# A transformer layer with PEER experts: the first 768 columns of `expert_v` multiplied densely with scattered weights, on one stream of 1280-column rows

## The reference

```
def peer_ffn(h, w_q, sub_keys_1, sub_keys_2, expert_u, expert_v):
    ...
    s1 = jnp.einsum('bshd,hnd->bshn', q[..., 0, :], sub_keys_1.astype(f32))
    s2 = jnp.einsum('bshd,hnd->bshn', q[..., 1, :], sub_keys_2.astype(f32))
    v1, i1 = lax.top_k(s1, PEER_TOPK)
    v2, i2 = lax.top_k(s2, PEER_TOPK)
    cand = (v1[..., :, None] + v2[..., None, :]).reshape(B, S, PEER_HEADS, PEER_TOPK * PEER_TOPK)
    ...
    top, pos = lax.top_k(cand, PEER_TOPK)
    eidx = jnp.take_along_axis(cidx, pos, axis=-1)
    gate = jax.nn.softmax(top, axis=-1)
    ...
        u = jnp.take(expert_u, idx, axis=0)
        act = jax.nn.gelu(jnp.einsum('td,tkd->tk', h_t, u), approximate=False)
        vv = jnp.take(expert_v, idx, axis=0)
        return jnp.einsum('tk,tkd->td', g * act, vv)
```

## Time and profile before

| | us |
|---|---|
| median of three runs | 2214.85 |
| the profiled execution | 2217.75 |
| its span | 2216.0 |
| VectorE busy | 1599.2 (72%) |
| TensorE busy | 1398.2 (63%) |
| POOL busy | 656.1 (30%) |
| ScalarE busy | 352.1 (16%) |
| DMA | 680.99 MB, mean 307 GB/s |

### The profile page before, as it was taken

How to read it: one execution, slowest core, us unless ns; L and a number is a source line. 1 busy time by engine, 2 the same in 40 slices (tenths; PEclk the granted TensorE clock), 3 DMA queues, 4 the chain that set the end, 5 groups by cost and what they waited for, 6 DMA issues and landing times.

```text
span 2216.0 us, 20313 instructions
## 1 busy us (share of the span) xinstructions
PE 1398.2 (63%) x7103; PEld 1192.1 (54%) x7103; DVE 1599.2 (72%) x2429; ACT 352.1 (16%) x702; POOL 656.1 (30%) x707
## 2 busy tenths in 40 slices
PE   4799999999998989999999990399000000000000
PEld 3688888888885468888888880398000000000000
DVE  5936555655664023777778669988899998999998
ACT  2022222222221011011111110276000000000000
POOL 1021332223321001333332446422433333333331
PEclk8889999999999999999999995699555555555555
DMA  9936554565455552799999999854999999999995
GB/s 397 385 132 242 228 196 177 213 254 226 175 191 226 214 206 94 292 344 360 361 357 357 363 407 411 328 149 125 422 422 421 422 422 421 422 422 422 422 422 243
DMA packets 122001, 680.99 MB, mean 307 GB/s; under 512 B 13488, under 2 KB 13616, under 8 KB 65840
## 3 DMA queue, kind: packets, MB, share of 16 engines
q0 software_dynamic: 73728, 419.46, 47.0%
q1 hardware_dynamic: 47760, 257.97, 30.5%
q10 hardware_dynamic: 416, 2.25, 0.2%
HBM read 675.44 MB, written 4.19 MB: 307 GB/s over the span
## 4 chain that ended last, share of the span: by engine, by line
PE 37%; DMA 30%; DVE 28%; issue 2%; ACT 1%; POOL 1%; DVEq 0%; ACTq 0%; POOLq 0%
DVE ps L1569 15%; DMA arena<-in_u_rows,arena 15%; DMA arena<-in_expert_v,arena 13%; PE ps L865 13%; PE ps L1186 5%; PE ps L914 5%; PE ps L943 4%; DVE arena L1523 3%; DVE arena L1235 2%; PE ps L1084 2%; PE ps L948 2%; DMA arena<-in_ada 1%; PE ps L957 1%; DVE arena L1463 1%; DVE arena L1458 1%
## 5 line engine op out<-in xcount | busy, mean ns | idle before, releaser
L1569 DVE SCALAR_TENSOR_TENSOR ps<-arena,ps 128x2048 f32<-128x2048 f32 x256 | 602.8, 2355 | 36.1 <-DMA arena<-in_expert_v,arena 5.7
L1158 PE MATMUL ps<-arena 128*128 128x256 f32 x1792 | 386.9, 379 | 0.0
L544 POOL DMA_INDIRECT arena<-in_u_rows,arena x256 | 245.9, 961 | 446.8 <-DVE arena L1523 393.1
L1158 PEld LDWEIGHTS ps<-arena 128*128 128x128 f32 x1792 | 340.4, 190 | 46.2
L544 POOL DMA_INDIRECT arena<-in_expert_v,arena x256 | 239.8, 937 | 410.5 <-DVE ps L1569 380.0
L865 PE MATMUL ps<-arena 128*128 128x256 f32 x1440 | 341.2, 381 | 2.8 <-DMA arena<-in_w_in 2.8
L1523 DVE SCALAR_TENSOR_TENSOR arena<-arena,ps 128x1152 f32<-128x1152 f32 x208 | 279.5, 1354 | 77.9 <-DMA arena<-in_u_rows,arena 73.4
L865 PEld LDWEIGHTS ps<-arena 128*128 128x128 f32 x1440 | 263.0, 191 | 33.0 <-issue 3.2
L1186 PE MATMUL ps<-arena 128*128 128x128 f32 x512 | 124.8, 399 | 88.6 <-DVE ps L1531 86.1
L1186 PEld LDWEIGHTS ps<-arena 128*128 128x128 f32 x512 | 98.8, 206 | 93.1 <-DVE ps L1531 86.3
L1214 DVE SCALAR_TENSOR_TENSOR arena<-arena 128x2048 f32<-128x2048 f32 x60 | 142.8, 2380 | 0.0
(11 more groups left out here) (246 smaller groups left out, 1579.1 us busy)
## 6 DMA issues: line engine op xcount, KB each, us to landing
arena<-in_ada SPq DMA_DIRECT2D x96, 1024.0 KB, 4.9
arena<-in_u_dense SPq DMA_DIRECT2D x128, 448.0 KB, 6.9
arena<-in_w_in SPq DMA_DIRECT2D x45, 1024.0 KB, 6.7
arena<-in_w_tail SPq DMA_DIRECT2D x32, 1024.0 KB, 6.9
arena<-in_w_in SPq DMA_DIRECT2D x12, 512.0 KB, 16.9
arena<-in_u_rows,arena POOLq DMA_INDIRECT x256, 9.0
arena<-in_expert_v,arena POOLq DMA_INDIRECT x256, 25.5
arena<-in_x ACTq DMA_DIRECT2D x1, 2048.0 KB, 15.0
```

Of the source, the lines that this page charges most:

```text
L544: nc.gpsimd.indirect_dma_start(out=row, out_offset=None, in_=table[:, :], in_offset=bass.IndirectOffsetOnAxis(ap=i32(idx[:, b, k:k + 1]), ...
L1158: last = mm(bank(5 + j % 2, 0, T), u_tile[j % len(u_tile)][:, k, :], h2T[:, k, :], start=(k == 0), stop=(k == KU - 1))
L1569: stt(sums_ps, v_row[n % len(v_row)], wv[:, b, k:k + 1], sums_ps, ALU.mult, ALU.add).then_inc(v_sum, 1)
```

## The change

`expert_v` gets what `expert_u` had. Its first 768 columns (`VD`) become 128 tiles of 128 experts, which are multiplied for all experts and both blocks (`v_product`, L1352 of the kernel after). For this the weights of a token's chosen experts must stand in an array over all 128 x 128 experts; they are scattered there by one-hots: for a token, the one-hot of its first keys times the weighted one-hot of its second keys, a matmul over the 128 places (`scatter`, L1327), four tokens a step in 64 steps `s`. ScalarE writes the result over `dense`, whose products of `u` for those tokens have been used (`scattered`, L843). For even `s` the first keys' one-hot is made by POOL (`nc.gpsimd.tensor_tensor`, L602) and two passes of ScalarE (L850, L852), for odd `s` by VectorE (L1730); the second keys' weighted one-hots are VectorE's, four instructions (L1733).

`KU` goes from 7 to 6, and `u` rows and `v` rows both have 1280 columns (`GU`) and share one stream of 512 rows through six slots (`ROWS`). The tiles too are one stream. Dots take `h` from SBUF throughout (L1701). Two dots stand in 10 of 14 gaps inside each of the last seven routes. The token step is turned round: `dense[:, :, t]` is now the weights and the one-hot the moving operand (L1289), so that tokens' products come out with the 128 places along the free axis; VectorE compares the second keys (spread as well, 256 columns instead of 128) and multiplies in one instruction of 128x512 (L1709), and TensorE sums over the partitions (`sum_up`, L1301). Per step stand two dots. From step 36 on (`HALF` + `LAG`) the scatters of block 0 run beside the steps of block 1. The sums of `v`'s rows are kept in SBUF (L1749).

```
@@ @@
-        hot = [view(repl_at, 4, P), view(repl_at + 4 * P, 4, P)]
...
+        row_slot = [new(GU) for _ in range(ROWS)]
...
+        h_row = [view(KU * T + b * GU, GU) for b in range(TB)]
+        v_acc = h_row
...
@@ @@
-            for j in range(4, NKEYS):
-                sp.wait_ge(tile_ps, j - 3)
+            for j in range(4, 2 * NKEYS):
+                sp.wait_ge(tile_ps, NKEYS if j in (NKEYS, NKEYS + 1) else j - 3)
+                if j == NKEYS + 2:
+                    sp.wait_ge(w_ps, T // 4)
                 product_tile(j)
...
@@ @@
+            for s in range(T // 4):
+                rows_to(rows_at_scatter(s))
+                if s == 0:
+                    pool.wait_ge(idxT_out, 1)
+                    pool.wait_ge(tile_ps, NKEYS)
+                if on_vector(s):
+                    continue
+                if s >= 2:
+                    pool.wait_ge(w_ps, s - 1)
+                nc.gpsimd.tensor_tensor(first_hot[s % 2], every_key(), first_keys(s), ALU.subtract).then_inc(key_gap, 1)
+            rows_to(2 * TB * KTOP)
...
@@ @@
+            def wanted(q):
+
+                if q >= 2:
+                    pe.wait_ge(prod_out, q - 1)
+                pe.wait_ge(hot_out, 2 * q + 2)
+                for i in range(4):
+                    last = mm(bank(4 + q % 2, i * P, (i + 1) * P), dense[:, :, 4 * q + i], hot[q % 2][:, i, :], start=True, stop=True)
+                last.then_inc(y_ps, 1)
...
+            def scatter(s):
+
+                if on_vector(s):
+                    pe.wait_ge(hot1_vec, s // 2 + 1)
+                else:
+                    pe.wait_ge(hot1_act, 2 * by_act(s))
+                pe.wait_ge(hot2_out, 4 * (s + 1))
...
+                if s >= 1:
+                    pe.wait_ge(w_out, s if s <= HALF else s - 1)
+                for i in range(4):
+                    last = mm(bank(scatter_bank(s), i * P, (i + 1) * P), first_hot[s % 2][:, i, :], second_hot[s % 2][:, i, :], start=True, stop=True)
+                last.then_inc(w_ps, 1)
...
             spread_keys(0)
             for q in range(T // 4):
                 if q + 1 < T // 4:
                     spread_keys(q + 1)
...
+                wanted(q)
+                if q:
+                    sum_up(q - 1)
...
+                if q >= HALF + LAG:
+                    scatter(q - HALF - LAG)
...
+            pe.wait_ge(w_out, T // 4)
+            for j in range(NKEYS):
+                pe.wait_ge(tile_land[place(NKEYS + j)], 16 * ((NKEYS + j) // len(tile_slot) + 1))
+                last = v_product(j, 0)
...
@@ @@
+            def wanted_products(q):
+
                 dve.wait_ge(y_ps, q + 1)
+                if q >= 2:
+                    dve.wait_ge(summed, q - 1)
+                dve.wait_ge(key2_out, q + 1)
+                stt(prod[q % 2], key2_h[q % 2], plus_p, bank(4 + q % 2).rearrange("p (a b) -> p a b", a=4),
+                    ALU.is_equal, ALU.mult).then_inc(prod_out, 1)
...
+            for q in range(HALF, 2 * HALF):
+                wanted_products(q)
+                if q == HALF + 1:
+                    activations(0)
+                more_dots(1)
...
+                if q >= HALF + LAG:
+                    weighted_one_hot(q - HALF - LAG)
+                if ndot[0] < TB * KTOP:
+                    more_dots(1)
+                else:
+                    v_sums(1)
...
+            for s in range(HALF, 2 * HALF):
+                weighted_one_hot(s)
+                if s % 2:
+                    v_sums(1)
```

More of the change, by code:

```diff
@@ new lines, in first_key @@
+            def first_key(s):
+                n = by_act(s)
+                act.wait_ge(key_gap, n)
+                nc.scalar.activation(first_hot[s % 2], first_hot[s % 2], ACT.Abs).then_inc(hot1_act, 1)
+                act.wait_ge(hot1_act, 2 * n - 1)
+                nc.scalar.activation(first_hot[s % 2], first_hot[s % 2], ACT.Relu, bias=ones[:, 0:1], scale=-1.0).then_inc(hot1_act, 1)
+            for q in range(T // 4):
+                one_hot(q)
+                if q == 0:
+                    act.wait_ge(idxT_ps, 1)
+                    nc.scalar.activation(idxT.rearrange("p a b -> p (a b)"), bank(7), ACT.Copy).then_inc(idxT_out, 1)
+                if q == HALF + 1:
+                    gelu(0)
+                if q == HALF + 2:
+                    turned_weights(0)
+                if q >= HALF + LAG and not on_vector(q - HALF - LAG):
+                    first_key(q - HALF - LAG)
+                if q > HALF + LAG:
+                    scattered(q - HALF - LAG - 1)
@@ new lines, in _ @@
+            for s in range(HALF - LAG, HALF):
+                if not on_vector(s):
+                    first_key(s)
+                scattered(s - 1)
+            scattered(HALF - 1)
+            first_key(HALF)
+            gelu(1)
+            turned_weights(1)
+            for s in range(HALF + 1, T // 4):
+                if not on_vector(s):
+                    first_key(s)
+                scattered(s - 1)
+            scattered(T // 4 - 1)
+            nc.scalar.preload_act_table_set("natural_log_exp_and_others")
@@ new lines, in _, with more_dots, two_dots @@
+            ndot, nstep = [0], [0]
+            def more_dots(count):
+                dots(ndot[0], min(ndot[0] + count, TB * KTOP))
+                ndot[0] = min(ndot[0] + count, TB * KTOP)
+            def two_dots():
+                nstep[0] += 1
+                if nstep[0] % 7 not in (3, 6):
+                    more_dots(2)
+            for c in range(1, 8):
+                route(c // 4, c % 4, two_dots)
+            for q in range(HALF):
+                wanted_products(q)
+                more_dots(2)
+                if q == HALF - 8:
+                    gate_sums(0)
@@ new lines, in _, with gathered_part @@
+            assert ndot[0] == TB * KTOP
+            for s in range(HALF - LAG, HALF):
+                weighted_one_hot(s)
+            activations(1)
+            v_sums(2)
+            weights(1)
+            v_sums(2)
+            for s in range(HALF, 2 * HALF):
+                weighted_one_hot(s)
+                if s % 2:
+                    v_sums(1)
+            v_sums(KTOP + KTOP // 2 - nsum[0])
+            def gathered_part(b):
+                dve.wait_ge(gw2_out, 1)
+                dve.wait_ge(row_used, (TB + b + 1) * KTOP)
+                tt(fb[b][:, VD:], v_acc[b], gw2[:, VD:], ALU.mult).then_inc(fin_v, 1)
@@ L1577, in _ @@
-                    dve.wait_ge(fin_v, 4 * b + 2 * h + 1)
-                    tt(xs[:, b, c], xs[:, b, c], ff[:, c], ALU.add).then_inc(fin_v, 1)
+                    stt(x1[:, b, c], fb[b][:, c], rstd[:, 12 + b:13 + b], x1[:, b, c], ALU.mult, ALU.add).then_inc(fin_v, 1)
+            v_sums(TB * KTOP)
+            dve.wait_ge(x_in, 48)
+            for b in range(TB):
+                gathered_part(b)
+                finish(b)
 NCONST = 40
```

375 lines of the change are left out of this document (232 added, 143 removed).

## The result

The changed kernel takes 2232.8 us (median of four runs, 2229.1 to 2236.0) against 2215.1 for the kernel before: a ratio of 1.0079, with a 95% interval of 1.0067 to 1.0092. The forecast was 2211, so it had the wrong sign, and lay 22 us short. The profiled execution took 2235.96 us, its span 2234.2.

A forecast was written before the change was run, and what follows sets the result against it. TensorE was taken to bound the product of `u`, VectorE the first token steps, an engine loop the late ones, DMA mostly the end; stages summed to a 2212 us span, plus 1.75, less 2.9: 2211, range 2140 to 2275.

The forecast's parts named there:

- the late loop: Last 28 token steps: VectorE and TensorE wait for each other in turn, 6.8 us a step with a dot, 6.1 without.
- the 42 MB: Fewer bytes of `u` and `v`, worth 103 us at 409 GB/s; expected to come back as idle DMA.
- the second product: Dense product of `v`: 330 us of matmuls; a rival at 1.2 GHz made its stage 655 us, total 2370, chance 0.03.
- first wanted product begins: Start of token steps: last route at 1232, product of `u` done at 1274, first wanted rows 5 us later, 1279.
- steps 0 to 35: First 36 token steps: VectorE sets 3.45 us each, 124 us, plus 3 for two gate sums and one Gelu.
- steps 36 to 63: Last 28 token steps, joined by scatters: 186 us, bounds 150 and 215, plus 14 for a low clock.
- 32 scatters in pairs: Scatters after the token steps: 4.6 us a pair, 74 us, plus 6 for the clock.
- product and rows of `v`: Last stage: DMA at 409 GB/s beside 330 us of matmuls, then 98 rows at VectorE's 1.66 us; 494 us.
- The hole: Before the first token step: VectorE stands still for some 45 us with six rows waiting.
- the forecast's own case: Whole kernel: 2211 us, -0.2%, case range 2190 to 2235, chance 0.45; faster 0.46 in all, slower 0.45.
- Rival 1: Token and scatter steps: strided weights load at 0.11 us and the clock holds; 2165 us, chance 0.23.
- Rival 2: Token and scatter steps: clock falls to 1.2 GHz, 66 us instead of 20, engines collide, some 6 more; 2263, chance 0.22.

The follow-up runs named there:

- the run with 18 dots: Changed kernel with 18 dots moved from the token steps into VectorE's wait before the product of `u` ends: 2203.01 us.
- the eleven kernels with the same early part: Follow-up kernels that leave the changed kernel's early part alone; in them and the changed kernel the product of `u` ended at 1275.4 to 1281.4 us.
- the best order: Changed kernel with one-hots ahead of the product, POOL's difference two gathers earlier, 18 dots ahead of token steps, all first-key one-hots on VectorE: 2139.00 us, ratio 0.9644.

## Why the prediction was wrong

Its mechanism held: the late loop was there piece by piece, the 42 MB came back as idle DMA, the second product ran at a granted clock of 0.99, and tiles kept TensorE waiting in it for 10.5 us only. The step that failed is the sum of the stages, 2212 for a span of 2234.2, and in it three terms that were too small: the end of the routes and with it the first wanted product (8 us), the steps around the first block's activations (7), and the last stage (6). In its own order, on the span's clock:

| part | forecast | measured |
|---|---|---|
| first wanted product begins | 1279 | 1286.9 |
| steps 0 to 35 | 127 | 133.7 |
| steps 36 to 63 | 200 | 204 |
| up to the pairs | 18 | 19.7 |
| 32 scatters in pairs | 80 | 77.5 |
| product and rows of `v` | 494 | 499.6 |
| tail | 14 | 12.9 |

(The first row is a point in time, each other row a length that is added to it; 204 is 28 times 7.28.) Every difference is 8 us or less, and all large ones have one sign.

- **The start (+8).** Routes came every 51.3 us, as forecast, but the last ended at 1242.4, not 1232 to 1235: only 20 dots had begun by 936 and 22 by 939, where I had 24, an estimate with no row behind it, and I had rounded down besides. Then 16 tiles, exactly as forecast: 1242.4 + 16 x 2.59 = 1283.8 against 1281.4, two being ready ahead. The hole behind it was there, 43 us, with VectorE busy for 3.5 of them; the forecast saw it, and the run with 18 dots shows it was worth 30 us. About half of the 8 us belongs to this one execution: in the eleven kernels with the same early part the first wanted product begins between 1281.0 and 1285.2.
- **Steps 0 to 35 (+7).** The step was right (3.48 against 3.45), the term beside it was not. The three steps around the first block's activations took 16.4 us and not 10.4: TensorE's sums wait for the addition (3.28 us), which waits behind two dots on VectorE, and the spread and the wanted rows wait behind the sums. I had priced the instructions at 3 us and not what is queued behind them.
- **Steps 36 to 63 (+4).** Two errors that nearly cancel. Four one-hots keep VectorE for 1.03 us (1507.88 to 1508.91), not 0.80: an instruction of 128 columns is issued every 0.26 us, and the rows I went from had 256. That is 6 us. ScalarE's evacuation with its strided write takes 1.05 us where I had 0.65. Against these the clock cost 9 us and not 14, and I had ScalarE in the chain of even steps, where it wasn't; the terms that I named for that chain add up to 5.4 us besides, and not to the 6.8 that I took. That the stage came out within 4 us is luck in part.
- **Pairs (-2).** 4.84 us for 4.6, but then I had added 6 us for a clock that costs nothing here.
- **Rows of `v` (+6).** Tiles and rows flowed at 408 GB/s as forecast, and the last 89 rows came at 1.66 us, as forecast too. But the product took 352 us, not 330: TensorE waited 12 us in it, 10.5 of them for tiles, did 32 matmuls more that the sum lacks (3.7 us), and began with some at half clock.

Behind the three terms stands one more step that failed, the one from this sum to a sign. The forecast stood 0.2% under the time before, and it had itself said that 4 us decide. Its terms were rounded from rows of other shapes, each to within some us, and six of them in a row make 10 to 20. The range (2140 to 2275) and the forecast's own case (2190 to 2235) knew that; the sign was a toss.

Rival 1, the lighter loop, failed on the stride (0.23 us, not 0.11). Rival 2 had the right sign for the wrong reason: the clock costs 9 us and not 66, and in the last stage POOL's collisions cost gathers time that nobody waits for. What was missed altogether is that the order could be changed. The gain was neither absent nor lost to contention: in the best order 78 of the 103 us that 42 MB are worth are there (2217 to 2139), though 21 of them come from filling a hole (2168 to 2147).

## What to carry to other kernels

A step that goes round several engines costs the sum of its parts, whatever each engine's busy share. Look in the program order for the instruction that stands behind a wait without needing it: here the one-hots behind the product, and POOL's difference behind two gathers. Two such loops can lie over each other, so that each repair alone gives little (16 and 3 us) and both give 64; what gave the second one away here was a step time that alternated at 4.5 and 9.4 us, though a clock that changes between its levels made steps alternate too (5.8 and 7.8). And a forecast nearer to the time before than the sum's own error has no sign to give.

## What the runs showed of the hardware

- Weight loads of 128 columns with a stride of 1 KB between fp32 elements start 0.22 us apart, contiguous ones 0.11; the operand that moves pays about the same. At half clock the difference is nearly gone: eight contiguous ones with their passes take 2.04 us, eight strided ones 2.09.
- ScalarE writes 128x512 with that stride in 1.05 us; contiguous, evacuations of that size take 0.60 (0.59 at L826, which writes bf16).
- VectorE's 128-column `tensor_scalar` with two pointers is issued every 0.26 us.
- POOL's gather beside a VectorE instruction that reads two SBUF operands takes 1.36 us and not 0.94, and a POOL instruction of 1.05 us lengthens such a VectorE instruction by 0.79 us. Beside a VectorE without gaps one gather took 27.38 us.
- The granted clock from 1440 to 1540 us was 0.85 in the changed kernel and 1.00 with unused matmuls in TensorE's gaps, which gave 9 us of 2233. With the one-hots ahead of the product TensorE was busier than in the changed kernel (73 of the 100 us for 64) and had 0.76.
